# Moving the modulation steps of a streamed transformer kernel: out of the hybrid tail, into the dense, Mamba and mixture blocks

## The chip, the cores and the metric

The kernel runs on one core of one Trainium2 chip. The metric is the device time of one execution in microseconds; a comparison goes by the median of several executions.

## The reference

For 256 tokens of width 1024, in fp32, two chains of layers are computed one after the other. Every layer but the last norm is modulated by the condition vector c:

```python
def adaln(c, w, b):
    mod = jax.nn.silu(c) @ w + b
    shift, scale, gate = jnp.split(mod[:, None, :], 3, axis=-1)
    return shift, scale, gate

def modulate(x, norm_w, shift, scale):
    return rmsnorm(x, norm_w) * (1 + scale) + shift

for layer in range(DEPTH):                 # DEPTH = 2
    if layer % 2 == 0:
        mix = hybrid_mixer(modulate(x, ...), ...)     # GLA and NSA heads
        x = x + gate * mix
        x = x + gate * swiglu(modulate(x, ...), dense_w_gu, dense_w_down)
    else:
        x = x + gate * mamba2_mixer(modulate(x, ...), ...)
        x = x + gate * moe_ffn(modulate(x, ...), router, w_gu, w_down)   # 8 experts, top 2
return rmsnorm(x, final_norm)
```

After it come two layers of the second chain, each with a norm, a projection of width 4096, dilated and block attention, an output projection and a gate. So there are six modulations, mod0 to mod5 (hybrid, dense, Mamba, mixture, and the two second layers). Each is the product of silu(c) (1024) with a matrix of 1024 by 3072: the first 2048 columns are shift and scale, the last 1024 the gate.

## The kernel before

All weights are streamed from memory once, in chunks of 512 KB (128 partitions by 1024 numbers), through one ring of six buffers, by DMAs that the queue of SyncE (SP) issues in the order in which they were asked for. A weight chunk is called a half: ScalarE rounds it to the short format of the matmul (`split_scalar`, L503), VectorE subtracts to get the rest (`split_vector`, L515), and TensorE forms three products of high and low parts for every matmul (`mm3`, L526 to L528). Rounding and subtracting run up to SPLITS = 6 halves ahead of TensorE (`m + SPLITS` in the calls). A half of the dense block, of its down part and of the projections is twelve to 24 matmuls, one of the mixture six.

The modulations are not computed by matmuls of the stream but on VectorE. A modulation step multiplies one chunk of its matrix (128 rows by 1024 columns) by the matching 128 values of silu(c), one value per partition, and adds to an accumulator `macc` (`back_vector`, L579; the first step of each part, L576, only multiplies). A modulation has 24 such steps: 16 for shift and scale ("step"), 8 for the gate ("gate"). What is left is the sum over the 128 partitions, by TensorE with a matrix of ones (`back_tensor`): a "sum" entry of 16 columns of blocks (32 instructions) and a "gates" entry of 8 (16 instructions), each borrowing a PSUM bank; VectorE then adds the bias (L589, L591, L596, L599). All entries of the six modulations stand in one list, `Stream.back` (L400 to L408), in the order in which they must run; a few are "rest", which do nothing. The list is not tied to times. Both engines walk it with `back_steps(engine, k, name, n, limit)`, called at fixed places in their programs, n entries per call, and `back_until` runs it up to a named entry. On TensorE an entry of kind step, gate or rest costs nothing. So moving calls moves every later entry, and with it the load of the chunk, which takes its place in SP's order where VectorE's program asks for it. A chunk's buffer is free again when its step has run.

Where the list is walked, before:

- the hybrid block: one entry per half of the projection; then its tail, in which only the attention and GLA tracks ("live") run, two entries per round of the tracks, up to mod1's "gates" entry (L1070, L1164). Then the output projection with its sum entries, four halves with one entry each;
- the dense block (`dense_tensor` L1753, `dense_vector` L1864): a stage of gate and up weights per item j (11 items of two tiles), with 0, 2, 1, 1 entries in its four parts (`dense_back`), and, per unit of four tiles, a down-stage of four halves with one entry at every second half. At the start of the block the list is run up to mod1's gates, and the gate, a column per block, is turned to a row (`row_tensor`, 16 small matmuls). TensorE's items take two of the banks 4 to 7 (`turns.take`), freed by VectorE's product of up and silu(gate) (`up_vector`, L1828), which is followed by the low part of the operand (L1833); VectorE and ScalarE do this for item j - 1 behind a split in the stage of item j. The list stops there at BACK_PAUSE, the first gate entry of mod4;
- the Mamba block (`mamba_tensor`, `mamba_vector`): one entry per quarter of the first four items of SSM_ORDER, beside the convolution (taps L2163, activation L2147);
- the mixture (`moe_tensor` L2336, `moe_vector` L2435): none. An expert is 14 items of four halves; after every second item comes a down-stage of four halves. After an item TensorE turns the gated product that VectorE writes (L2688) with two transposes (`flip_tensor`), and the gather of the next expert runs from item 8 on;
- the second layers (`second_tensor` L3006, `second_vector`): one entry per quarter of the rounds (part 0 and 1, items i = 0 to 3), for layer 0 and for the part of layer 1 that still has entries. The last norms have fill matmuls (`norm_tensor`, NORM_FILL, `fill`): matmuls on constants whose result nobody reads, in place of idle time.

## Time and profile before

| | |
|---|---|
| time, median of 3 executions | 2112.31 us (2109.10 to 2114.84) |
| the profiled execution | 2110.27 us, span 2108.5 us |
| mean granted TensorE clock | 0.982 of full |
| TensorE (matmul) busy | 2007.5 us, 95% |
| VectorE busy | 1718.7 us, 82% |
| ScalarE busy | 1321.8 us, 63% |
| DMA | 560.19 MB, mean 266 GB/s |

The page of the profile gives the busy time per engine and the groups of instructions that cost most, each with its idle time before it and what ended that. Then the waits per engine and line say who waits for whom. The timeline of an engine, over a few microseconds, shows a line per run of like instructions, with the idle time ahead of it in brackets; the window table gives busy time, granted clock and DMA rate of a stretch. Names: `ring` is the buffer of a streamed chunk, `sph` and `spl` its high and low part, `ps` a PSUM bank, `macc` the accumulator of the modulations, `hH`, `hL`, `rH`, `rL` the high and low parts of operands, `arena` scratch. The blocks lie at about 30 to 228 us (hybrid), 230 to 440 (dense), 440 to 700 (Mamba), 720 to 1730 (mixture), 1730 to 1925 and 1925 to 2105 (second layers).

### The profile page before, as it was taken

The numbers are of one execution on the slowest core, as the hardware profiler recorded it, in microseconds if no ns is written. First come the engines' busy times: TensorE is split into PE (matmuls) and PEld (weight loads), VectorE is DVE, ScalarE is ACT, GpSimd is POOL, SyncE is SP. The second block draws the span as 40 slices with busy tenths as digits, with TensorE's granted clock in tenths as the row PEclk, the third lists the DMA queues.
The fourth block names the chain that finished last, engine by engine and source line by source line (L and its number), as shares of the span: only waits on it lengthen the run. The fifth ranks groups of instructions, "written<-read, shape, count | busy, mean of one in ns | idle before, by whom it ended". The sixth has DMA issues, their size and how long they took to land.

```text
span 2108.5 us, 28640 instructions
## 1 busy us (share of the span) xinstructions
PE 2007.5 (95%) x10424; PEld 1663.2 (79%) x10424; DVE 1718.7 (82%) x2427; ACT 1321.8 (63%) x1972; POOL 0.2 (0%) x4
## 2 busy tenths in 40 slices
PE   6998999998989999999999999999999999999997
PEld 5777889978877788888888888888788866767776
DVE  7688878768777698989899898998989988776664
ACT  4354534355564688778787777777778764544543
POOL 0000000000000000000000000000000000000000
PEclk9999999999999999999999999999999999999999
DMA  9846688846332399989999998999989984662530
GB/s 371 294 146 214 240 295 316 292 145 203 127 102 97 107 377 337 359 320 369 358 354 355 329 366 324 377 348 334 364 322 370 364 331 173 214 213 93 197 110 20
DMA packets 154211, 560.19 MB, mean 266 GB/s; under 512 B 17232, under 2 KB 17488, under 8 KB 153936
## 3 DMA queue, kind: packets, MB, share of 16 engines
q1 hardware_dynamic: 154064, 558.29, 72.6%
q8 instruction: 85, 1.39, 0.3%
q14 instruction: 62, 0.51, 0.1%
HBM read 557.18 MB, written 1.05 MB: 265 GB/s over the span
## 4 chain that ended last, share of the span: by engine, by line
PE 74%; DVE 14%; ACT 6%; issue 3%; DMA 3%; DVEq 0%; SPq 0%; ACTq 0%
PE ps L526 20%; PE ps L528 20%; PE ps L527 20%; PE ps L532 11%; DVE spl L515 7%; PE ps L536 3%; ACT sph L503 2%; DVE macc L579 1%; DMA ring<-in_moe_gu 1%; DMA ring<-in_dense_down 1%; DMA ring<-in_mod 1%; DMA ring<-in_moe_down 1%; ACT arena L2129 1%; ACT arena L770 1%; DVE arena L2163 0%
## 5 line engine op out<-in xcount | busy, mean ns | idle before, releaser
L515 DVE TENSOR_TENSOR spl<-ring,sph 128x1024 fp32r<-128x1024 f32 x906 | 1077.5, 1218 | 274.4 <-ACT sph L503 265.2
L503 ACT ACTIVATE sph<-ring 128x1024 fp32r<-128x1024 f32 x906 | 949.3, 1059 | 554.1 <-PE ps L528 407.5
L526 PE MATMUL ps<-sph,hH 128*128 128x512 f32 (+1 forms) x1296 | 520.3, 401 | 1.3 <-DVE hL L883 1.3
L528 PE MATMUL ps<-sph,hL 128*128 128x512 f32 (+1 forms) x1296 | 507.2, 391 | 0.0
L527 PE MATMUL ps<-spl,hH 128*128 128x512 f32 (+1 forms) x1296 | 505.8, 390 | 0.0
L526 PEld LDWEIGHTS ps<-sph,hH 128*128 128x128 f32 x1296 | 245.5, 189 | 51.5 <-issue 3.8
L528 PEld LDWEIGHTS ps<-sph,hL 128*128 128x128 f32 x1296 | 244.7, 189 | 52.5
L527 PEld LDWEIGHTS ps<-spl,hH 128*128 128x128 f32 x1296 | 245.5, 189 | 48.0 <-issue 1.0
L526 PE MATMUL ps<-sph,rH 128*128 128x512 f32 x664 | 269.9, 407 | 5.6 <-ACT arena L3117 2.0
L528 PE MATMUL ps<-sph,rL 128*128 128x512 f32 x664 | 260.8, 393 | 0.0
L527 PE MATMUL ps<-spl,rH 128*128 128x512 f32 x664 | 260.7, 393 | 0.0
L526 PE MATMUL ps<-hH,sph 128*128 128x256 f32 x640 | 185.7, 290 | 5.5 <-DVE arena L1182 3.6
L528 PE MATMUL ps<-hH,spl 128*128 128x256 f32 x640 | 183.1, 286 | 0.0
L527 PE MATMUL ps<-hL,sph 128*128 128x256 f32 x640 | 183.0, 286 | 0.0
L532 PE MATMUL ps<-arena 128*128 128x128 f32 (+6 forms) x940 | 147.7, 302 | 15.8 <-DVE arena L2322 9.2
L579 DVE SCALAR_TENSOR_TENSOR macc<-ring,st,macc 128x1024 f32<-128x1024 f32 x124 | 158.0, 1278 | 4.2 <-DMA ring<-in_mod 3.0
L526 PEld LDWEIGHTS ps<-sph,rH 128*128 128x128 f32 x664 | 126.0, 190 | 37.2 <-issue 3.1
L532 PEld LDWEIGHTS ps<-arena 128*128 128x128 f32 (+2 forms) x940 | 120.5, 194 | 39.9 <-issue 26.9
L536 PE MATMUL ps<-cst,arena 128*128 128x128 f32 (+2 forms) x640 | 114.5, 288 | 37.3 <-DVE arena L2688 13.1
L528 PEld LDWEIGHTS ps<-sph,rL 128*128 128x128 f32 x664 | 125.6, 189 | 27.3
L527 PEld LDWEIGHTS ps<-spl,rH 128*128 128x128 f32 x664 | 126.0, 190 | 25.5 <-issue 1.4
L536 PEld LDWEIGHTS ps<-cst,arena 128*128 128x128 f32 (+2 forms) x640 | 81.0, 147 | 80.6 <-issue 30.8
(313 smaller groups left out, 1766.9 us busy)
## 6 DMA issues: line engine op xcount, KB each, us to landing
ring<-in_moe_gu SPq DMA_DIRECT2D x448, 512.0 KB, 5.4
ring<-in_moe_down SPq DMA_DIRECT2D x224, 512.0 KB, 5.3
ring<-in_mod SPq DMA_DIRECT2D x144, 512.0 KB, 4.8
ring<-in_w_in SPq DMA_DIRECT2D x64, 512.0 KB, 4.3
ring<-in_dense_gu SPq DMA_DIRECT2D x44, 512.0 KB, 5.5
ring<-in_ssm_w_in SPq DMA_DIRECT2D x40, 512.0 KB, 3.4
ring<-in_dense_down SPq DMA_DIRECT2D x22, 512.0 KB, 5.6
ring<-in_hyb_w_in SPq DMA_DIRECT2D x20, 512.0 KB, 5.9
```

Source lines behind the costliest of these rows:

```text
L503: a.activation(k.high[m % SPLITS][:, 0:w], raw[:, 0:w], ACT.Copy).then_inc(k.S.half_rounded, 1)
L515: v.tensor_tensor(k.low[m % SPLITS][:, 0:w], raw[:, 0:w], k.high[m % SPLITS][:, 0:w], ALU.subtract).then_inc(*k.tick(k.S.half_split, f"hal ...
L526: pe.matmul(out, a[0], b[0], start=start, stop=False, skip_group_check=True)
L527: pe.matmul(out, a[0], b[1], start=False, stop=False, skip_group_check=True)
L528: return pe.matmul(out, a[1], b[0], start=False, stop=stop, skip_group_check=True)
L532: return pe.matmul(out, a, b, start=start, stop=stop, skip_group_check=True)
L536: return pe.transpose(out, in_, k.C["ident"][0:n, 0:n])
L579: v.scalar_tensor_tensor(out=m, in0=w[:, :], scalar=c, in1=m, op0=ALU.mult, op1=ALU.add).then_inc(*tick(S.mod_stepped, f"mod{i}.step{r}"))
L770: a.activation(k.norm_space.fulls[2 * t + h][:, j, :], bank[:, j * 128:(j + 1) * 128], ACT.Identity, bias=k.mods[:, i, c:c + 1], scale=k.m ...
L2129: a.activation(conv_slot(k, f), bank, ACT.Identity, bias=k.V["convb"][:, f:f + 1], scale=cw[:, f, 3:4]).then_inc(*tick(S.conv_in, f"ssm{j} ...
```

## The change

The list is the same but for one thing: mod1, like mod4, has three "rest" entries ahead of its sum, and its gate steps all come behind the sum. What moves are the calls:

- The hybrid tail stops at mod1's first gate entry instead of its "gates" entry. By the counts of the entries, ten steps run later than before.
- The gate's row of the dense block is not made at its start but behind item GATE_AT = 2 (list up to mod1's gates, then `gate_tensor` on banks 2 and 3 and `gate_scalar`), and the norm before has two fills in its place.
- The down-stages of the dense block call entries (0, 2, 1, 1) on TensorE and one per half on VectorE, so four per unit instead of two. In them the up product of VectorE and its part on ScalarE stand ahead of the split of the first half, not behind. The two fills ahead of the last down-stage go.
- In the Mamba block, the last quarter of an item has no entry, and the first item has two per quarter.
- The mixture has one entry per expert, behind item BACK_AT = 11.
- In the second layers, quarters 2 and 3 of the rounds with i = 1 have none.

In number of VectorE steps: ten fewer in the hybrid tail, eight more in the dense block, two more in the Mamba block, eight in the mixture, eight fewer in the second layers. The amount of arithmetic is unchanged, apart from four fill matmuls more at one place and four fewer at another.

```diff
--- before.py
+++ after.py
@@ -400,7 +400,7 @@
         self.back = []
         for i in range(6):
             steps, gates = [("step", i, r) for r in range(2 * KD)], [("gate", i, 2 * KD + r) for r in range(KD)]
-            late = [("rest", i, r) for r in range(3)] if i == 4 else gates[0:3]
+            late = [("rest", i, r) for r in range(3)] if i in (1, 4) else gates[0:3]
             if i == 0:
                 self.back += steps[0::2] + [("shift", 0, 0)] + steps[1::2] + [("sum", 0, 0)] + gates
                 continue
@@ -710,6 +710,8 @@
             fill(pe, k, banks, NORM_FILL[i])
     if i > 3:
         fill(pe, k, banks, 6 if i == 5 else 3)
+    if i == 1:
+        fill(pe, k, banks, 2)
     if i == 0:
         back_steps(pe, k, "tensor", 5)
         fill(pe, k, k.banks_turn, 1)
@@ -1067,7 +1069,7 @@
             live.append(gla_tensor(pe, k, linear, one))
     while live:
         advance(live)
-        back_steps(pe, k, "tensor", 2, ("gates", 1, 0))
+        back_steps(pe, k, "tensor", 2, ("gate", 1, 2 * KD))
     k.back_banks = one
     pe.wait_ge(*when("hyb.low2"))
     m = k.stream.first["hyb_out"]
@@ -1161,7 +1163,7 @@
             live.append(gla_vector(v, k))
     while live:
         advance(live)
-        back_steps(v, k, "vector", 2, ("gates", 1, 0))
+        back_steps(v, k, "vector", 2, ("gate", 1, 2 * KD))
     v.wait_ge(*k.when("dtw.high"))
     v.tensor_tensor(k.dtw3[:, :, 32:64], k.dtw[:, :, :], k.dtw3[:, :, 0:32], ALU.subtract).then_inc(*k.tick(k.S.vector_step, "dtw.low"))
     v.wait_ge(*k.when("row3.high"))
@@ -1750,12 +1752,14 @@
 
 
 
+
+GATE_AT = 2
+
+
 def dense_tensor(pe, k):
     S, tick, when = k.S, k.tick, k.when
     norm_tensor(pe, k, 1, k.banks_turn.only(4, 5, 6, 7))
     turns = k.back_banks = k.banks_turn.only(4, 5, 6, 7)
-    back_until(pe, k, "tensor", 1, "gates")
-    row_tensor(pe, k, "ffn.gate", k.mods[:, 1, 16:24], 8, ("mod1.gated",))
     acts = [[x[:, i * 1024:(i + 1) * 1024].rearrange("p (k n) -> p k n", k=4) for x in (k.rH, k.rL)] for i in range(2)]
     us, tail = units(DENSE_TILES), []
     for u in range(-1, len(us)):
@@ -1777,10 +1781,12 @@
                                            [x[:, n, :] for x in (k.hH, k.hL)], n == 0 and r == 0, n == 7)
                     last.then_inc(k.S.half_used, 1)
                     dense_back(pe, k, "tensor", part)
+                if j == GATE_AT:
+                    back_until(pe, k, "tensor", 1, "gates")
+                    for _ in gate_tensor(pe, k, "ffn", 1, k.banks_turn.only(2, 3)):
+                        pass
         if u >= 0:
             f, nt = us[u]
-            if u == len(us) - 1:
-                fill(pe, k, turns, 2)
             pe.wait_ge(*when(f"act{f + nt - 1}.low"))
             for kk in range(nt):
                 m = k.stream.at["dense_down", f // 2 + kk // 2] + kk % 2
@@ -1793,8 +1799,7 @@
                         out_banks(pe, k, "ffn", t)
                     last = out_product(pe, k, w, acts[u % 2], kk, t, f + kk == 0, False)
                 last.then_inc(k.S.half_used, 1)
-                if kk % 2 == 0:
-                    back_steps(pe, k, "tensor", 1, BACK_PAUSE)
+                back_steps(pe, k, "tensor", (0, 2, 1, 1)[kk], BACK_PAUSE)
     out_tail(pe, k, "ffn", tail)
 
 
@@ -1835,7 +1840,6 @@
 
 def dense_scalar(a, k):
     norm_scalar(a, k, 1)
-    row_scalar(a, k, "ffn.gate", k.F.gate, 8)
     us = units(DENSE_TILES)
     done = 0
     for u in range(-1, len(us)):
@@ -1847,6 +1851,9 @@
                     if part == 0 and done < j:
                         up_scalar(a, k, done)
                         done += 1
+                if j == GATE_AT:
+                    for _ in gate_scalar(a, k, "ffn", k.F.gate):
+                        pass
         if u == 0:
             rope_scalar(a, k)
         if u >= 0:
@@ -1854,16 +1861,15 @@
             for kk in range(nt):
                 if f + kk >= DENSE_TILES - 4:
                     break
-                split_scalar(a, k, k.stream.at["dense_down", f // 2 + kk // 2] + kk % 2 + SPLITS)
                 if kk == 0 and done < DENSE_TILES // 2 and k.stream.at["dense_gu", done] < k.stream.at["dense_down", f // 2]:
                     up_scalar(a, k, done)
                     done += 1
+                split_scalar(a, k, k.stream.at["dense_down", f // 2 + kk // 2] + kk % 2 + SPLITS)
     squares_scalar(a, k, "ffn", k.stream.first["ssm"], 2)
 
 
 def dense_vector(v, k):
     norm_vector(v, k, 1, "hyb")
-    back_until(v, k, "vector", 1, "gates")
     us = units(DENSE_TILES)
     done = 0
     for u in range(-1, len(us)):
@@ -1876,6 +1882,8 @@
                         up_vector(v, k, done)
                         done += 1
                     dense_back(v, k, "vector", part)
+                if j == GATE_AT:
+                    back_until(v, k, "vector", 1, "gates")
         if u == 0:
             rope_vector(v, k)
         if u >= 0:
@@ -1883,12 +1891,11 @@
             for kk in range(nt):
                 if f + kk >= DENSE_TILES - 4:
                     break
-                split_vector(v, k, k.stream.at["dense_down", f // 2 + kk // 2] + kk % 2 + SPLITS)
-                if kk % 2 == 0:
-                    back_steps(v, k, "vector", 1, BACK_PAUSE)
                 if kk == 0 and done < DENSE_TILES // 2 and k.stream.at["dense_gu", done] < k.stream.at["dense_down", f // 2]:
                     up_vector(v, k, done)
                     done += 1
+                split_vector(v, k, k.stream.at["dense_down", f // 2 + kk // 2] + kk % 2 + SPLITS)
+                back_steps(v, k, "vector", 1, BACK_PAUSE)
     add_vector(v, k, "ffn", k.stream.first["ssm"], k.F.gate, ("ffn.gate.copied4",), k.F.tmp, 2)
 
 
@@ -1929,8 +1936,8 @@
                                    c == 0, c == 7)
             last.then_inc(S.half_used, 1)
             advance(live)
-            if j in SSM_ORDER[0:4]:
-                back_steps(pe, k, "tensor", 1, BACK_PAUSE)
+            if j in SSM_ORDER[0:4] and q < 3:
+                back_steps(pe, k, "tensor", 2 if j == SSM_ORDER[0] else 1, BACK_PAUSE)
             if scan_starts(j, q):
                 live.append(scan_tensor(pe, k, beside))
         if j >= 4:
@@ -1996,8 +2003,8 @@
         for q in range(4):
             split_vector(v, k, m + q + SPLITS)
             advance(live)
-            if j in SSM_ORDER[0:4]:
-                back_steps(v, k, "vector", 1, BACK_PAUSE)
+            if j in SSM_ORDER[0:4] and q < 3:
+                back_steps(v, k, "vector", 2 if j == SSM_ORDER[0] else 1, BACK_PAUSE)
             if scan_starts(j, q):
                 live.append(scan_vector(v, k))
         if j >= 4:
@@ -2333,6 +2340,10 @@
 
 
 
+
+BACK_AT = 11
+
+
 def moe_tensor(pe, k):
     S, tick, when, E = k.S, k.tick, k.when, k.E
     norm_tensor(pe, k, 3, k.banks_turn.only(4, 5, 6, 7))
@@ -2383,6 +2394,8 @@
         if it == 8 and e + 1 < N_EXP:
             gather_now_tensor(pe, k, e + 1)
             live.append(gather_tensor(pe, k, e + 1))
+        if it == BACK_AT and e < N_EXP:
+            back_steps(pe, k, "tensor", 1)
         if it in (3, 6) and 1 <= e < N_EXP:
             scatter_tensor(pe, k, e - 1, it // 3 - 1)
     fill(pe, k, k.banks_turn, 3)
@@ -2469,6 +2482,8 @@
             shares_vector(v, k, e + 1)
         if it == 8 and e + 1 < N_EXP:
             live.append(gather_vector(v, k, e + 1))
+        if it == BACK_AT and e < N_EXP:
+            back_steps(v, k, "vector", 1)
         if it in (3, 6) and 1 <= e < N_EXP:
             live.append(scatter_vector(v, k, e - 1, it // 3 - 1))
         while q >= n_items - 1 and live:
@@ -3029,7 +3044,8 @@
                         last = second_product(pe, k, m, q, t, outs[t])
                     last.then_inc(k.S.half_used, 1)
                     advance(live)
-                    back_steps(pe, k, "tensor", 1)
+                    if i != 1 or q < 2:
+                        back_steps(pe, k, "tensor", 1)
             if part == 1 and i == 0:
                 back_until(pe, k, "tensor", 4 + l, "gates")
                 live.append(gate_tensor(pe, k, f"s{l}", 4 + l, beside))
@@ -3174,7 +3190,7 @@
             for q in range(4):
                 split_vector(v, k, m + q + SPLITS)
                 advance(live)
-                if part + i > 0:
+                if part + i > 0 and (i != 1 or q < 2):
                     back_steps(v, k, "vector", 1)
             if part == 1 and i == 0:
                 back_until(v, k, "vector", 4 + l, "gates")
```

## Rows read from the trace of the kernel before

**Rows 1.** The page: busy time by engine, and the chain of waits.

```profile
PE 2007.5 (95%) x10424; PEld 1663.2 (79%) x10424; DVE 1718.7 (82%) x2427; ACT 1321.8 (63%) x1972; POOL 0.2 (0%) x4
...
PE 74%; DVE 14%; ACT 6%; issue 3%; DMA 3%; DVEq 0%; SPq 0%; ACTq 0%
```

**Rows 2.** The page, costliest groups: count, busy, mean ns, idle before.

```profile
L515 DVE TENSOR_TENSOR spl<-ring,sph 128x1024 fp32r<-128x1024 f32 x906 | 1077.5, 1218 | 274.4 <-ACT sph L503 265.2
...
L503 ACT ACTIVATE sph<-ring 128x1024 fp32r<-128x1024 f32 x906 | 949.3, 1059 | 554.1 <-PE ps L528 407.5
...
L579 DVE SCALAR_TENSOR_TENSOR macc<-ring,st,macc 128x1024 f32<-128x1024 f32 x124 | 158.0, 1278 | 4.2 <-DMA ring<-in_mod 3.0
```

**Rows 3.** Windows table: length, busy us by engine (instructions), PEclk, DMA share, GB/s.

```profile
272.60:276.00 3.40, 3.35 (x15) 3.35 (x16) 2.73 (x5) 1.69 (x3) 0.00 (x0) 0.50 1.00 407
...
1965.60:1969.00 3.40, 3.40 (x11) 2.85 (x11) 2.84 (x3) 0.60 (x1) 0.00 (x0) 0.50 0.80 263
```

**Rows 4.** PE timeline, dense block: start, us, line, tiles, count, [idle before].

```profile
272.65 1.22 PE L532 MATMUL ps<-cst,macc 128*128 128x128 f32 x4 [2.07 <-DVE arena L1828]
...
313.05 0.71 PE L532 MATMUL ps<-cst,macc 128*128 128x128 f32 x4 [1.04 <-DVE arena L1828]
...
421.80 1.88 PE L532 MATMUL ps<-cst 128*128 128x512 f32 x4
424.48 0.50 PE L526 MATMUL ps<-sph,rH 128*128 128x512 f32 x1 [0.80 <-DVE rL L1833]
```

**Rows 5.** DVE timeline, hybrid tail.

```profile
187.82 1.28 DVE L579 SCALAR_TENSOR_TENSOR macc<-ring,st,macc 128x1024 f32<-128x1024 f32 x1
...
191.39 2.66 DVE L579 SCALAR_TENSOR_TENSOR macc<-ring,st,macc 128x1024 f32<-128x1024 f32 x2
```

**Rows 6.** PE timeline, start of the output projection and of the dense block.

```profile
195.31 0.50 PE L526 MATMUL ps<-sph,rH 128*128 128x512 f32 x1 [1.50 <-DVE rL L1225]
...
230.03 0.36 PE L526 MATMUL ps<-hH,sph 128*128 128x256 f32 x1 [1.02 <-DVE hL L883]
```

**Rows 7.** PE timeline, the sum before the last norm.

```profile
1920.93 3.73 PE L532 MATMUL ps<-cst,macc 128*128 128x128 f32 x32
```

**Rows 8.** DVE timeline, Mamba block.

```profile
473.72 1.28 DVE L579 SCALAR_TENSOR_TENSOR macc<-ring,st,macc 128x1024 f32<-128x1024 f32 x1
```

**Rows 9.** PE timeline, Mamba block.

```profile
477.03 0.30 PE L536 MATMUL ps<-cst,arena 128*128 128x128 f32 x1 [2.84 <-ACT arena L2147]
...
508.62 0.44 PE L536 MATMUL ps<-cst,arena 128*128 128x128 f32 x2 [1.07 <-DVE mods L589]
```

**Rows 10.** Windows table, a stretch of the mixture, columns of rows 3.

```profile
950.00:966.00 16.00, 16.00 (x74) 13.18 (x73) 15.47 (x17) 13.71 (x18) 0.00 (x0) 1.00 1.02 407
```

**Rows 11.** DVE timeline, mixture, the gated product.

```profile
961.06 0.41 DVE L2688 TENSOR_TENSOR arena<-arena,ps 128x256 f32<-128x256 f32 x1
```

**Rows 12.** PE timeline, mixture, the turns that take it.

```profile
962.45 0.38 PE L536 MATMUL ps<-cst,arena 128*128 128x128 f32 x2
```

**Rows 13.** All waits: engine, line, releaser: us in total, times, longest.

```profile
PE ps L536 <- DVE arena L3276: 6.5, 4, 1.9
```

**Rows 14.** PE timeline, second block.

```profile
1780.36 1.42 PE L536 MATMUL ps<-cst,arena 128*128 128x128 f32 x8 [1.84 <-DVE arena L3276]
...
1808.49 0.91 PE L532 MATMUL ps<-cst,macc 128*128 128x128 f32 x3 [1.31 <-DVE arena L1685]
...
1865.61 0.44 PE L536 MATMUL ps<-cst,arena 128*128 128x128 f32 x2
...
2034.23 1.03 PE L536 MATMUL ps<-cst,arena 128*128 128x128 f32 x6 [0.89 <-DVE arena L3276]
```

**Rows 15.** DVE timeline, second block.

```profile
1867.58 0.47 DVE L1685 SCALAR_TENSOR_TENSOR arena<-cst,ps 128x128 f32<-128x128 f32 x2
```

**Rows 16.** Windows table, a dense unit and an expert, as rows 3.

```profile
332.00:366.00 34.00, 34.00 (x242) 32.10 (x242) 28.10 (x30) 15.05 (x21) 0.00 (x0) 1.00 0.91 334
968.10:1094.10 126.00, 124.20 (x575) 102.21 (x575) 114.42 (x128) 99.72 (x127) 0.00 (x0) 1.00 0.93 349
```

## The prediction

> **What bounds the kernel now.** I first read the busy shares [rows 1]: TensorE 95%, VectorE 82%, and a chain of waits that is 74% TensorE, 14% VectorE and 3% DMA. The costliest groups with the idle time ahead of them [rows 2] say which of them is ahead: ScalarE's rounding of the weights (L503) waits 407.5 us for TensorE to use up a half, and VectorE's subtraction (L515) 265.2 us for that rounding. So the splitting of the streamed weights mostly runs ahead, six halves at most, and the end is set by TensorE. A microsecond taken off VectorE is worth something only where TensorE waits for that very operation, and one added costs something only where VectorE is late. Two quantities therefore carry the sum: TensorE's idle gaps, and the stretches at the lower of its two clocks [rows 3]: granted clock 0.50, that is 1.2 instead of 2.4 GHz, for 3.4 us each, each right behind an idle gap. The first lies behind the gap of 2.07 us that ends at 272.65 [rows 4]. Work that fills such a stretch takes twice as long, so it costs 3.4 / 2 = 1.7 us on top of the gap. Not every gap has one: behind the 1.04 us that end at 313.05 the same four matmuls took 0.71 us, behind the 2.07 us 1.22 [rows 4].
>
> The prices of the moved pieces: a modulation step takes VectorE 1.28 us, of which 0.08 overlap the next operation (so 1.20 in a queue), a weight split 1.22 [rows 2]. Each step also brings one 512 KB load on SP's queue, in the same ring of buffers as the weights: it holds a buffer until the step has run, and the weight loads asked for after it come one place later. Ten steps fewer in the tail, eight more in the dense block, two more in the Mamba block, eight in the mixture and eight fewer in the second block mean so many loads each; their number stays.
>
> **The hybrid tail.** Before, the tail's rounds issue two back-list entries each; the change stops at mod1's gates, so ten steps leave. The step at 187.82 stands between the sum and the attention's last operations; two more, at 191.39 to 194.05 [rows 5], stand ahead of the subtraction that makes the mixer's low part (L1225), for which TensorE waits 1.50 us before the output projection at 195.31 [rows 6]. One step of 1.2 us off the first chain and two off the second would be 3.7 us; TensorE's own transposes, which end 1.50 us before 195.31, are then next and move forward by the first of the steps alone: 1.5 + 1.2 = 2.7, less a little of the low clock that they run at, so I take 2.5 (bounds 1.5 and 3.1).
>
> **Entering the dense block.** The gate's 16 small matmuls and the row's 16 matmuls moved behind item 2. Before, the row's matmuls were followed by a wait for the normed input that runs on for 1.02 us more, to 230.03 [rows 6], so they were free; fills take their place. After, the row stands on the path, 16 of the small matmuls of which 32 take 3.73 us [rows 7]: -1.8. mod1's gates cost TensorE about as much in item 1 as they did in the output projection (16 such again), 0. Item 2's bank is taken later because VectorE's product now follows a split: -0.8. With the tail: 2.5 - 1.8 - 0.8 = **-0.1** (bounds -2.5 and +1.5).
>
> **Sums in the dense block.** TensorE waits 2.07 us at 272.65 and 1.04 us at 313.05 for a bank that VectorE's product L1828 frees [rows 4]; the first is followed by the low clock [rows 3]. That is 2.07 + 1.6 + 1.04 = 4.7 us. After, eight steps more run in the block (two entries more per down-stage), the products stand ahead of the splits, and the sums fall elsewhere: sum 2 at item 5, gates 2 at the start of item 6. One such wait of 1 to 2 us stays, I think, perhaps with a slow stretch: **+2.4** (1.0 to 4.0).
>
> **End of the dense block.** Four fill matmuls (1.88 us) and then 0.80 us of waiting for rL L1833 [rows 4]. The fill goes, and the operand is ready earlier since the product no longer waits behind a split: **+2.7** (if VectorE is still late, only 0.8 to 1.5 of it, since a removed fill then merely becomes idle time).
>
> **The Mamba block.** One step ends up ahead of the convolution's taps at 473.72 [rows 8], and TensorE waits 2.84 us at 477.03, with the low clock behind it; at 508.62 it waits 1.07 us for a sum's copy [rows 9]. After, the last quarter of each item has no step: 1.2 off the first wait, 1.1 off the second, and the slow stretch may go: 1.2 + 1.1 + 1.2 (of 1.7) = **+3.5** (2.3 to 4.0).
>
> **The mixture.** This is new work beside a tight loop: eight steps, one per expert after item 11's down splits. Around there the transfers are saturated (407 GB/s, DMA share 1.02, [rows 10]), one chunk of 524,288 bytes every 1.29 us. VectorE's gated product (L2688) ends at 961.06 + 0.41 = 961.47 and TensorE takes it at 962.45 without waiting: slack 0.98 us [rows 11, 12]. A step in front costs VectorE 1.20 and the chunk delays what lands behind it by one 1.29: per expert from 1.20 - 0.98 = 0.2 to 1.20 + 1.29 - 0.98 = 1.5 us. The upper end is a step that runs only after the late half; but VectorE can do it while that half lands, and then 1.29 - 0.98 = 0.3 is lost. I take 0.6, nearer to this overlap: 8 x 0.6 = **-5** (0 if the splits' lead covers it, -12 if nothing overlaps).
>
> **The second block.** Rounds 2 and 3 of item 1 lose their steps. TensorE's turns wait four times for VectorE's L3276, 6.5 us in all [rows 13]: 1.84 at 1780.36, 0.89 at 2034.23 where no steps run [rows 14], so 3.8 us in the two between, near 1853 and 1965. If these fall to 0.85 to 0.9 each, that is 3.8 - 1.75 = +2.05, and with the slow stretch at 1965.6 [rows 3], 1.65 of its 1.7, +3.7. The waits of 1.84 and of 1.31 at 1808.49 (for gates 4, [rows 14]) are each followed by a slow stretch too; the first shortens to 0.6 without its clock, the second moves behind the turns, 2.5 and its clock: 1.84 + 1.7 + 1.31 + 1.6 - 0.6 - 2.5 - 1.7 = +1.6 (-1 to +3). Against that, sum 5, 3.73 us at 1920.93 before a norm that waits anyway [rows 7], is now reached earlier in the list and lands in a saturated round: 3.75 us, plus a wait for a bank of pair 6, 7 until VectorE's L1685 ends at 1867.58 + 0.47 = 1868.05 [rows 15] (TensorE has its transposes behind it at 1865.61 + 0.44 = 1866.05, [rows 14]: 2.0), plus a slow stretch, 1.6: -7.4 (-5.8 if the clock holds). The norm's gap, now empty for 3.7 us, then lowers the clock for the turns behind it: -1.5 (0 to -3). Together 3.7 + 1.6 - 7.4 - 1.5 = **-3.6** (-7 to 0).
>
> **Sum.** -0.1 + 2.4 + 2.7 + 3.5 - 5 - 3.6 = -0.1 us saved. The profiled execution took 2110.27 us, 2.04 under the median 2112.31; 2110.3 + 0.1 + 2.0 gives **2112.3 us**. Its own range from the bounds, taken not all at once, is 2106 to 2118.
>
> **Rivals.**
> First, faster: no slack is missing in the mixture (0 instead of -5), sum 5 keeps its clock (+1.6), and the norm's fill keeps the clock (+1.5): 2112.3 - 8.1 = 2104, down to 2100. For it speaks that ScalarE is 407.5 us ahead as a whole [rows 2]; against it, the saturated transfers of [rows 10]. Chance 0.29.
> Second, slower, by one mechanism: the mixture's step delays the product by more than its 0.98 us of slack in every expert, and the half behind the chunk too. It decides from that 0.98 on: 8 x 1.5 = 12 instead of 5, which gives 2119.3; where the wait goes on to lower the clock once or twice, 2122. For it: VectorE is busy 15.47 of 16 us there [rows 10]; against: the step can run while the late half lands. Chance 0.20.
> Third, the transfers bind. A dense unit took 34 us, and its 334 GB/s are 21.7, so 22 chunks (12 halves, 10 steps); an expert took 126 us, and its GB/s are 84 chunks [rows 16]. Now they are 24 and 85. At 1.29 us [rows 10] that is 31.0 and 109.7 us, so they don't bind and it costs nothing. Were the expert's mean pace of 126 / 84 = 1.50 us all that there is, a unit would take 36.0 us, 2 longer, five times, and each expert 1.5 longer, 12 for the 5: 2112.3 + 10 + 7 = 2129. The window of [rows 10] speaks against it. Chance 0.03. By the Trainium skill's page "DMA: Bandwidth & Descriptors", section "Where 436 GB/s comes from", the memory side of a core is limited to about 358 GB/s, from which I estimate 1.46 us per chunk and 35.1 us for a dense unit; this trace disagrees, with 407 GB/s over 16 us.
> Fourth, the edits do not do what they say: steps pushed out of the tail simply come back where TensorE waits equally, so that all terms cancel: 2112, within 2. Chance 0.02.
>
> **Chances.** The forecast has 0.46. A measurement of this kernel tells about 0.3% (6.3 us) from no change. Faster by more than that (under 2106): 0.27 of the first rival and 0.04 of the forecast, 0.31. Slower (over 2118.6): 0.17 of the second, 0.03 of the third and 0.03 of the forecast, 0.23. The rest, 0.46, lies within. The range takes in the first rival to 2101 and the second to 2121, which leaves about a tenth on either side.
>
> **What would show it.** Right: no wait at the output projection's start near 193, no fill and no wait ahead of the last down-stage, waits at 474 and 508 shorter by 1.2 and 1.1; in the mixture a wait of 0.2 to 1.5 us at item 13 of each expert, ended by L2688; a sum of 32 instructions in the saturated round near 1867 with a wait ahead of it. Wrong: experts as long as before (126 us) would take the 5 us away; a norm 5 without the low clock 1.5; a sum 5 that is found elsewhere 7.4; expert lengths over 127.3 us would be the second rival; and dense units over 35 us the third.

## The result, and the profile after

The changed kernel takes 2117.43 us (median of 20 executions, 2110.41 to 2122.49) against 2109.35 us of the kernel before beside it (20 executions, 2102.70 to 2114.84): a ratio of 1.0034, 95% interval 1.0024 to 1.0044. It is slower by a third of a per cent, about 7 us. The prediction had said no change, 2112.3 us.

The profiled execution of the changed kernel took 2116.84 us, span 2115.1. Its page, for the busy time and the chain of waits:

```profile
PE 2003.9 (95%) x10424; PEld 1658.6 (78%) x10424; DVE 1718.6 (81%) x2427; ACT 1322.5 (63%) x1972; POOL 0.2 (0%) x4
...
PE 67%; DVE 17%; ACT 7%; DMA 6%; issue 3%; DVEq 0%; SPq 0%; ACTq 0%
```

TensorE's busy time fell by 3.6 us and VectorE's is the same as in [rows 1], so nothing is paid in work. What changed is the chain: TensorE's share of it went from 74 to 67%, VectorE's from 14 to 17%, and the DMAs' from 3 to 6%. By this chain, moved loads hold up TensorE more often.

Where the time went can be read without any model. Every kernel here issues the same 7800 weight matmuls (lines 526 to 528) in the same order, so the start of the n-th one can be laid beside that of the kernel before. The differences by stage, in us (a stage runs from the first weight matmul of one to the first of the next; "low" is the time at granted clock 0.5 in it):

| stage | before | low | changed | low | difference |
|---|---|---|---|---|---|
| hybrid block with its output projection | 193.8 | 17.1 | 191.2 | 20.5 | -2.6 |
| dense block up to its last four down halves | 194.4 | 3.4 | 198.5 | 6.8 | +4.1 |
| those four and the norm | 28.9 | 3.3 | 27.5 | 0.5 | -1.4 |
| Mamba block | 270.9 | 20.8 | 270.5 | 20.2 | -0.4 |
| mixture | 999.0 | 0.0 | 1006.9 | 0.0 | +7.9 |
| end of the mixture, norm 4 | 25.9 | 6.8 | 25.3 | 0.0 | -0.6 |
| first second layer, with norm 5 | 184.3 | 13.7 | 188.6 | 13.7 | +4.3 |
| last layer | 166.5 | 10.2 | 162.3 | 3.5 | -4.2 |

The mixture alone is as large as the whole loss. The changed kernel's timeline of TensorE at the places that the prediction spoke of (start, length, line, tiles, count, idle time before and what ended it):

```profile
192.08 0.79 PE L526 MATMUL ps<-sph,rH 128*128 128x512 f32 x1 [0.56 <-DVE rL L1227]
...
227.08 0.36 PE L526 MATMUL ps<-hH,sph 128*128 128x256 f32 x1 [1.09 <-DVE hL L885]
...
250.19 1.95 PE L532 MATMUL ps<-cst,macc 128*128 128x128 f32 x16
...
253.61 0.39 PE L526 MATMUL ps<-hH,sph 128*128 128x256 f32 x1 [1.47 <-DVE mods L596]
...
310.72 2.07 PE L532 MATMUL ps<-cst,macc 128*128 128x128 f32 x8 [3.87 <-DVE arena L1833]
```

The output projection starts at 192.08 instead of 195.31 (the first row of [rows 6]), after 0.56 us of waiting instead of 1.50. The last row is what replaced the two waits of [rows 4]: one of 3.87 us.

The granted clock at these places and around the last norms, in the table of windows (length, busy time of each engine, clock, DMA share, GB/s):

```profile
189.70:196.50 6.80, 6.24 (x19) 4.88 (x19) 2.54 (x5) 2.24 (x5) 0.00 (x0) 0.50 0.00 0
309.20:316.00 6.80, 5.28 (x25) 5.28 (x25) 3.78 (x6) 2.11 (x5) 0.00 (x0) 0.50 0.88 337
...
1872.50:1875.90 3.40, 3.40 (x18) 3.40 (x18) 0.00 (x0) 0.00 (x0) 0.00 (x0) 0.50 0.53 176
1933.50:1937.30 3.80, 0.36 (x3) 0.36 (x4) 3.56 (x12) 0.52 (x3) 0.00 (x0) 1.00 0.28 109
```

And in the second layers:

```profile
1785.64 1.25 PE L536 MATMUL ps<-cst,arena 128*128 128x128 f32 x8 [0.65 <-DVE arena L3292]
...
1789.17 2.50 PE L532 MATMUL ps<-cst,macc 128*128 128x128 f32 x16 [2.27 <-DVE arena L3294]
...
1857.29 0.93 PE L536 MATMUL ps<-cst,arena 128*128 128x128 f32 x5 [0.74 <-DVE arena L3292]
...
1871.56 5.47 PE L532 MATMUL ps<-cst,macc 128*128 128x128 f32 x32 [2.07 <-DVE arena L1687]
...
1936.94 1.60 PE L536 MATMUL ps<-cst,arena 128*128 128x128 f32 x8 [3.69 <-DVE arena L869]
```

The sum of mod5 stands at 1871.56: 2.07 us of waiting and 5.47 us for 32 instructions that took 3.73 in [rows 7], since the low clock of 1872.5 lies over them. Norm 5 now waits 3.69 us where the sum had been.

### The profile page after: what moved, and what is told of

It is laid out like the page before. It is cut to its first block, busy times and chain, and to the rows that moved or that the text cites. A ratio compares the mean times of both kernels' runs of the same rounds, so it can differ in the third digit from the quotient of the medians.

```text
span 2115.1 us, 28639 instructions
## 1 busy us (share of the span) xinstructions
PE 2003.9 (95%) x10424; PEld 1658.6 (78%) x10424; DVE 1718.6 (81%) x2427; ACT 1322.5 (63%) x1972; POOL 0.2 (0%) x4
## 4 chain that ended last, share of the span: by engine, by line
PE 67%; DVE 17%; ACT 7%; DMA 6%; issue 3%; DVEq 0%; SPq 0%; ACTq 0%
PE ps L526 18%; PE ps L528 17%; PE ps L527 17%; PE ps L532 11%; DVE spl L515 9%; ACT sph L503 3%; PE ps L536 3%; DMA ring<-in_moe_down 3%; DMA ring<-in_moe_gu 2%; DVE macc L579 1%; DMA ring<-in_mod 1%; DVE arena L2170 1%; DMA ring<-in_dense_gu 1%; DVE arena L2703 0%; ACT arena L2136 0%
## 5 line engine op out<-in xcount | busy, mean ns | idle before, releaser
L526 PE MATMUL ps<-sph,rH 128*128 128x512 f32 x664 | 270.6, 408 | 4.5 <-ACT arena L3133 2.0
L527 PEld LDWEIGHTS ps<-spl,rH 128*128 128x128 f32 x664 | 126.4, 190 | 25.5 <-issue 1.4
```

The costliest lines, as they stand in the source:

```text
L526: pe.matmul(out, a[0], b[0], start=start, stop=False, skip_group_check=True)
L527: pe.matmul(out, a[0], b[1], start=False, stop=False, skip_group_check=True)
```

## The experiments

All ratios are to the kernel before, of the same batch, with their 95% intervals. The stages of all of them, as above, in us, each from one profiled execution:

| kernel | hybrid | dense | + norm | Mamba | mixture | norm 4 | layer 1 | layer 2 |
|---|---|---|---|---|---|---|---|---|
| before | 193.8 | 194.4 | 28.9 | 270.9 | 999.0 | 25.9 | 184.3 | 166.5 |
| changed | 191.2 | 198.5 | 27.5 | 270.5 | 1006.9 | 25.3 | 188.6 | 162.3 |
| x1, no mixture steps | 193.2 | 198.7 | 27.3 | 270.6 | 1000.2 | 25.5 | 178.0 | 164.9 |
| x2, sum 5 held | 190.0 | 198.0 | 27.3 | 270.7 | 1006.5 | 25.4 | 178.2 | 166.1 |
| x3, two steps per down-stage | 189.4 | 190.3 | 29.1 | 270.3 | 1004.1 | 28.1 | 184.1 | 166.4 |
| x4, order and fills alone | 196.6 | 189.3 | 30.0 | 270.8 | 999.8 | 26.0 | 184.1 | 164.9 |
| y1, steps spread in the items | 189.8 | 194.7 | 29.7 | 272.5 | 999.3 | 25.8 | 184.1 | 166.4 |
| y2, Mamba block's calls alone | 195.1 | 193.0 | 27.5 | 270.3 | 998.6 | 25.8 | 184.2 | 165.1 |
| y3, short operation | 193.7 | 198.7 | 27.5 | 270.4 | 1008.7 | 25.6 | 189.9 | 162.3 |
| y4, short load | 191.2 | 198.6 | 30.3 | 271.1 | 1005.6 | 25.0 | 189.6 | 160.6 |
| y5, mixture steps at item 7 | 189.6 | 198.7 | 30.1 | 270.0 | 1001.8 | 25.5 | 188.5 | 162.4 |
| z1, y3 and y4 together | 187.7 | 196.9 | 28.5 | 268.3 | 1010.1 | 26.0 | 188.5 | 162.2 |
| z4, y1 with free banks | 191.5 | 194.7 | 30.2 | 268.3 | 999.9 | 24.6 | 184.1 | 166.5 |
| z5, y5 and x2 | 189.9 | 197.3 | 28.5 | 268.4 | 1001.4 | 26.1 | 179.4 | 166.0 |

Rows that should agree show how far one profile can be trusted: the mixture without steps 998.6 to 1000.2, the hybrid stage of the changed kernel's code 187.7 to 193.7, by where the low clock falls.

### The mixture's steps: are they the loss?

```diff
-        if it == BACK_AT and e < N_EXP:
-            back_steps(pe, k, "tensor", 1)
...
-                    if i != 1 or q < 2:
-                        back_steps(pe, k, "tensor", 1)
+                    back_steps(pe, k, "tensor", 1)
```

(and the same for VectorE)

> The changed kernel without its eight steps in the mixture; the second layers get their steps in all quarters back, as before. Theory: in the changed kernel TensorE falls behind the kernel before by 8.1 us within the mixture (its weight matmuls start 0.98 us earlier than before at 593 us and 7.17 us later at 1730 us), and each step is the cause of that. Without them the mixture keeps the distance that it enters with, about -1 us, and the run ends about 1 us under before (between -3 and +1). Rival: the loss comes from a changed order of the ring's loads that the earlier blocks leave behind, not from the steps; then the mixture still loses 6 to 8 us and the run ends 5 to 8 us over before.

Measured: 2107.22 us, ratio 0.9977 (0.9961 to 0.9992). The mixture takes 1000.2 us: 6.7 of its 7.9 us are gone. The rival falls. The run is better than the theory said, 4.9 instead of 1 us under before, because of the first second layer, 178.0 us against 184.3. That is not the edit: its list and its waits there are those of the kernel before, and only the clock differs, as the part on the hardware below shows. About 6 of this profile's gain are therefore the clock's, and it isn't this execution alone: the median of the granted clock is 0.982 in its eight executions and 0.980 in the 29 of before (the table at the end).

### What does a step cost there: the operation, the load, or its place?

TensorE's waits for the gated product between 720 and 1735 us (us in total, times, longest), first of the kernel before, then of the changed one, and then item 13 of the second and the third expert in the changed kernel:

```profile
PE ps L536 <- DVE arena L2688: 13.1, 14, 1.2
```

```profile
PE ps L536 <- DVE arena L2703: 18.3, 21, 1.4
```

```profile
962.99 0.41 PE L536 MATMUL ps<-cst,arena 128*128 128x128 f32 x2 [0.65 <-DVE arena L2703]
...
1090.73 0.41 PE L536 MATMUL ps<-cst,arena 128*128 128x128 f32 x2 [1.37 <-DVE arena L2703]
```

Seven waits more for eight steps, and 5.2 us more of waiting out of the 7.9 lost. The first of the two shown stands where [rows 12] had none, and both are as long as the prediction had them (0.2 to 1.5). To tell apart what makes them, seven of the eight steps were cut down, one respect at a time (what these three kernels compute for mod4's gate is then not the reference's, and each was executed once):

```diff
-            v.scalar_tensor_tensor(out=m, in0=w[:, :], scalar=c, in1=m, ...)
+            n_ = 64 if i == 4 and kind == "gate" else QUARTER
+            v.scalar_tensor_tensor(out=m[:, 0:n_], in0=w[:, 0:n_], scalar=c, in1=m[:, 0:n_], ...)
```

> The changed kernel with seven of the eight modulation steps in the mixture working on 64 of their 1024 columns (the rest of that gate's sums is left out): VectorE's time for them almost goes, their loads stay. The stretch from the first to the last weight matmul of the mixture takes 999.0 us in the kernel before and 1006.9 in the changed one. Theory A, VectorE's own 1.2 us per step are the cost: it falls to 999 to 1001. Theory B, the load that delays the halves behind it by 1.29 us is the cost: it stays at 1005 to 1007.

Measured: the mixture takes 1008.7 us, 3.5 us of it at the low clock, which costs 1.7; without that 1007.0. The short operation (0.28 us instead of 1.28) has saved nothing. Theory A falls.

```diff
-        k.stream.ask(("mod", i, r), mod[r], QUARTER, f"mod{i}.step{r}")
+        slim = 64 if i == 4 and kind == "gate" and r != 2 * KD else QUARTER
+        k.stream.ask(("mod", i, r), mod[r][:, 0:slim], slim, f"mod{i}.step{r}")
```

> The changed kernel with seven of the eight modulation chunks in the mixture cut to 64 of 1024 columns in the load alone (the step works on whole rows of the buffer, so its result is not the reference's): VectorE's time stays, the transfer almost goes. Theory A (VectorE's time): the mixture stays at 1005 to 1007 us. Theory B (the load): it falls to 999 to 1001. If both halves of the cost count, each of the two runs lies in between, near 1003.

Measured: 1005.6 us. The short load saves 1.3 of 7.9 us. Theory B, that the transfer is the cost, falls too (the prediction had charged the operation and the transfer together).

> The changed kernel with seven of the eight mixture steps short in both respects: 64 of 1024 columns loaded and 64 worked on (that gate's sums are not the reference's). What is left of a step is its place in the ring of six buffers and in SP's and VectorE's order. With the short operation alone the mixture took 1008.7 us, with the short load alone 1005.6, as it stood 1006.9, without steps 999.0 to 1000.2. Theory C, the place is the cost (a buffer that holds no weights, so that the loads run one half less ahead in the stretch in which they catch up): 1004 to 1007. Theory D, operation and load hide each other's absence, either alone is enough to make the product late: 999 to 1002.

Measured, with both cuts: 1010.1 us, with 3.5 us of low clock, so 1008.4 without; the waits for the gated product are 20.0 us. Theory D falls, and C is what is left: neither the operation nor the bytes are the cost, so by elimination it is the place in the ring and in the order of loads. ScalarE's rounding in this kernel, behind the shortened load of the second expert:

```profile
948.89 1.06 ACT L503 ACTIVATE sph<-ring 128x1024 fp32r<-128x1024 f32 x1 [0.32 <-DMA ring<-in_moe_gu]
950.50 1.06 ACT L503 ACTIVATE sph<-ring 128x1024 fp32r<-128x1024 f32 x1 [0.55 <-DMA ring<-in_moe_gu]
952.73 1.06 ACT L503 ACTIVATE sph<-ring 128x1024 fp32r<-128x1024 f32 x1 [1.17 <-DMA ring<-in_moe_down]
954.42 1.06 ACT L503 ACTIVATE sph<-ring 128x1024 fp32r<-128x1024 f32 x1 [0.64 <-DMA ring<-in_moe_down]
```

It waits 1.17 us for a half although almost no bytes stood ahead of it, and the starts are 1.61, 2.23 and 1.69 us apart, where at the 407 GB/s of [rows 10] one half lands every 1.29. A half takes 5.4 us from issue to landing (the page's median), and a buffer is loaded again only when its step has run. That shows in the changed kernel at the second expert's step: SP issues its load, VectorE runs the step, and SP issues the load six places later into the same buffer.

```profile
948.26 0.33 SPq L485 DMA_DIRECT2D ring<-in_mod  x1
```

```profile
954.78 1.28 DVE L579 SCALAR_TENSOR_TENSOR macc<-ring,st,macc 128x1024 f32<-128x1024 f32 x1
```

```profile
956.09 0.33 SPq L485 DMA_DIRECT2D ring<-in_moe_down  x1
```

The step ends at 956.06 and the load is issued 0.03 us later; so it is at all eight steps. The buffer was away from the weights for 7.8 us. With both cuts it still was, for 7.0 us (issue at 943.27, end of the step at 950.27), because a load of a sixteenth of the bytes took 4.4 us instead of 5.2 (the medians of the modulation's loads in this kernel's list of DMAs) and the step waits its turn behind VectorE's splits. With one of six buffers holding no weights for so long, too few loads are under way to follow each other without a gap in the stretch in which the stream catches up. This last link is argued from the rows, no run varied the number of buffers.

```diff
-BACK_AT = 11
+BACK_AT = 7
```

> The changed kernel with the mixture's step behind item 7 instead of item 11. Theory: what it costs depends on where VectorE and the transfers are late; items 11 to 13 lie in the stretch in which the loads catch up after the gather of the next expert, item 7 lies ahead of the gather. The mixture then takes 999 to 1002 us instead of 1006.9, and the run is 4 to 7 us faster than the changed kernel. Rival: VectorE is equally full in every item, so each step costs its 1 us anywhere: 1005 to 1007.

Measured: 2110.95 us, ratio 1.0007 (0.9992 to 1.0023), mixture 1001.8 us, waits for the gated product:

```profile
PE ps L536 <- DVE arena L2703: 15.0, 15, 1.5
```

Fifteen waits instead of 21. The same eight steps cost 1.6 to 3.2 us ahead of the gather (over the 998.6 to 1000.2 without them) and 6.7 to 8.3 in the catching up behind it. The theory holds.

### The dense block: how many loads beside a down-stage?

In the changed kernel ScalarE waits for the down halves just ahead of the wait of 3.87 us:

```profile
302.16 1.06 ACT L503 ACTIVATE sph<-ring 128x1024 fp32r<-128x1024 f32 x1 [2.78 <-DMA ring<-in_dense_down]
305.46 1.06 ACT L503 ACTIVATE sph<-ring 128x1024 fp32r<-128x1024 f32 x1 [2.24 <-DMA ring<-in_dense_down]
308.02 1.06 ACT L503 ACTIVATE sph<-ring 128x1024 fp32r<-128x1024 f32 x1 [1.50 <-DMA ring<-in_dense_down]
```

Their starts are 3.30 and 2.56 us apart: a down half and a step's chunk take turns, each 1.29 us of transfer at the pace of [rows 10]. VectorE's product waits in its queue behind the splits of these halves, and it frees the bank that mod2's sum borrows.

```diff
-                back_steps(pe, k, "tensor", (0, 2, 1, 1)[kk], BACK_PAUSE)
+                if kk % 2 == 0:
+                    back_steps(pe, k, "tensor", 1, BACK_PAUSE)
```

> The changed kernel with two steps instead of four in each down-stage of the dense block (as before), and the second layers' steps in all quarters, which take up those that are left. The mixture's steps stay. Theory: in the changed kernel TensorE waits 3.87 us at 310.7 us for a bank, after ScalarE waited 2.78, 2.24 and 1.50 us for three down halves whose loads stand behind the steps' loads; the low clock behind it costs 2.6 us more. With two steps per stage that wait is at most 2 us and the dense block ends 4 to 6 us earlier; the mixture still loses 6 to 8 us; the run ends 1 to 4 us over before. Rival: the wait comes from where the sum falls, not from the number of loads; then it stays at 3 us or more and the dense block wins less than 2 us.

(The same on VectorE, and the second layers have their steps in all quarters again. In this kernel the steps of mod4 that are left over run in the mixture on an accumulator that holds other rows there, so the last layers' modulation is not the reference's.) Measured: 2108.97 us, ratio 0.9986 (0.9972 to 0.9999). The dense block takes 190.3 us instead of 198.5, more than the 4 to 6 expected: 1.9 of it is mod3's gates entry, which falls into the Mamba block, 3.4 the 6.8 us of low clock that are missing, and the rest the wait. The whole run is 3 us under before where 1 to 4 over was expected, and its mixture, with its steps, takes 1004.1 us, 1 under the least expected. TensorE's waits in the block (230 to 430 us) are then

```profile
PE ps L526 <- DVE mods L596: 1.5, 1, 1.5
```

and none for the product any more. By its own mark, a wait of 3 us or more that stays, the rival falls. But this kernel doesn't part the two theories by itself, since with fewer calls mod2's sum moves too: it stands behind the 1128th weight matmul, in the changed kernel behind the 1104th. The kernels with two steps per down-stage and an entry at that very place help. Before, mod2's gates stand behind the 1104th and wait 1.04 us for the same product [rows 4]; in x4 below, which has the product ahead of the split as the changed kernel has it,

```profile
313.33 2.05 PE L532 MATMUL ps<-cst,macc 128*128 128x128 f32 x16 [0.58 <-DVE arena L1826]
```

0.58 us, against 3.87 with four. So the place alone doesn't make the wait, and the number of loads beside it is what differs.

```diff
-                split_vector(v, k, ... dense_down ...)
-                if kk % 2 == 0:
-                    back_steps(v, k, "vector", 1, BACK_PAUSE)
                 if kk == 0 and done < DENSE_TILES // 2 and ...:
                     up_vector(v, k, done)
                     done += 1
+                split_vector(v, k, ... dense_down ...)
+                if kk % 2 == 0:
+                    back_steps(v, k, "vector", 1, BACK_PAUSE)
...
-            if u == len(us) - 1:
-                fill(pe, k, turns, 2)
```

> The kernel before with two edits of the change alone: in the down-stages the product stands ahead of the split, and the two fills ahead of the last down-stage are gone. Theory: the 1.88 us of fills and the 0.80 us of waiting at 424 us both go, and the waits for the product at 272 and 313 us shorten by a split each: 3 to 5 us under before. Rival: the fills covered a wait that is there anyway: the last down-stage starts at most 1 us earlier, and the run is within 1 us of before.

Measured: 2109.21 us, ratio 0.9992 (0.9979 to 1.0005), 1.7 us under before and not clear of it. That is less than the 3 to 5 of the theory. The dense stage does take 189.3 instead of 194.4 us, 1.7 of which are a low stretch that is missing, and the last down-stage starts with neither fill nor wait, so the rival falls; the waits for the product became 1.63 and 0.58 us instead of 2.07 and 1.04. But the stages on either side are 2.8 and 1.1 us longer, with 6.8 and 2.2 us more of low clock. The part works where it is made; as a whole it can't be told from the clock's scatter by the time alone. With the low clock taken out (the table at the end) it is worth 3.6 us.

```diff
-def dense_back(e, k, name, part):
-    back_steps(e, k, name, (0, 2, 1, 1)[part], BACK_PAUSE)
+def dense_back(e, k, name, part, j):
+    back_steps(e, k, name, (1 if j > 1 else 0, 2, 1, 1)[part], BACK_PAUSE)
```

(the same on VectorE, on top of x1 and x3)

> The changed kernel without steps in the mixture, two steps per down-stage as before, and instead one step more in the first quarter of the dense block's items 2 to 10; the second layers as before. Theory: what hurt in the dense block was four extra loads beside the four halves of a down-stage with the list's sum right behind it; spread over the items, the steps cost little: the dense block takes 190 to 193 us (194.4 before, 198.5 changed, 190.3 with two steps per down-stage and no others), and the run is 5 to 9 us under before. Rival: the block as a whole has no room for the loads (nine chunks in an item's 11.5 us are the full pace of 1.28 us): dense 196 us or more, and the run is no better than without the mixture's steps alone, 5 us under before.

Measured: 2105.40 us, ratio 0.9971 (0.9953 to 0.9988), 6.1 us under before. The dense block takes 194.7 us, over the 190 to 193 of the theory and under the rival's 196; the work is that of the changed kernel's 198.5. What spreading took away is above all the wait of 3.87 us and the low clock behind it: x1 and the changed kernel have 6.8 us of low clock in the stage, 3.4 us of time, and y1 has none. Without that the stage takes 195.1 to 195.3 us concentrated, 194.7 spread and 192.7 in the kernel before. So the steps aren't free anywhere in the block: ScalarE still waits 21.3 us for the items' loads (15.2 before), and TensorE has a new wait of 1.5 us for the copy of mod2's sum (L589).

(on top of y1)

```diff
-    turns = k.back_banks = k.banks_turn.only(4, 5, 6, 7)
+    turns, k.back_banks = k.banks_turn.only(4, 5, 6, 7), k.banks_turn.only(2, 3)
...
+                    k.back_banks = turns        # behind item GATE_AT
```

> The kernel with the steps spread over the dense block's items and none in the mixture, and with mod1's gates entry borrowing one of the banks 2 and 3, which nobody uses yet, instead of one of the items' four. Theory: TensorE's wait of 1.4 us for the copy of the gates (L596) behind the entry is a wait for a bank that the next item needs, so it goes with the bank: dense block 193.3 instead of 194.7 us, the run 1.4 us faster than with the spread alone, 6 to 8 us under before. Rival: the item then waits for its own product as long: nothing gained, 5 to 6 us under before.

Measured: 2104.40 us, ratio 0.9970 (0.9954 to 0.9985). The gates entry stands alone now,

```profile
250.93 1.95 PE L532 MATMUL ps<-cst,macc 128*128 128x128 f32 x16
```

with no wait before or behind it, and the block's waits are 3.7 instead of 4.9 us; so the wait for L596 was one for a bank. The stage is as long as in y1 (194.7), since a low stretch of 3.5 us lies in it, and the ratio can't be told from that of y1. The mechanism is shown, a gain in time is not.

### The second layers and the Mamba block

```diff
-                        back_steps(pe, k, "tensor", 1)
+                        back_steps(pe, k, "tensor", 1, ("sum", 5, 0) if l == 0 else None)
```

> The changed kernel, but the walk of the list in the first of the second layers stops in front of mod5's sum, which then runs ahead of the last norm, as before. Theory: the sum costs 7.4 us where the changed kernel has it (2.07 us of waiting for a bank at 1869 us, 3.75 us of work, 1.6 us of low clock) and is free in the norm's gap, where TensorE now waits 3.7 us: 5 to 7 us faster than the changed kernel, 0 to 2 us over before. Rival: the entries behind the sum, three gate steps, now fall into the next layer beside its own work and cost there what was won, and the wait for a bank goes to another borrower: under 3 us faster than the changed kernel, 4 or more over before.

Measured: 2109.78 us, ratio 0.9993 (0.9980 to 1.0005): from 1.0034 by 0.41%, 8.7 us, 4 to 14 from end to end of the two intervals, where 5 to 7 were expected. TensorE at norm 5:

```profile
1918.94 3.73 PE L532 MATMUL ps<-cst,macc 128*128 128x128 f32 x32
1922.51 2.74 PE L532 MATMUL ps<-cst 128*128 128x512 f32 x6
1925.37 1.09 PE L536 MATMUL ps<-cst,arena 128*128 128x128 f32 x8
```

Sum, fills and turns follow each other, and nothing waits. Layer 1 is 10.4 us shorter, 5.2 of it by 10.3 us less of low clock; layer 2 gives 3.8 back, of which 1.7 by the clock and 1.9 by a wait for a bank at mod5's gates. So the rival saw one thing rightly, and the theory holds; 3.5 of the 6.6 us that the two layers gained are the clock's.

> The changed kernel with two places mended: the mixture's step behind item 7, and mod5's sum held for the norm's gap. Theory: both gains add, since they lie in different blocks: 5 us from the mixture (1001.8 instead of 1006.9 us) and 6 us from the second layers, 2117.4 - 11 = 2106, that is 3 to 5 us under before. Rival: one of them comes back elsewhere, and the run is not clearly faster than before (within 2 us).

Measured: 2105.11 us, ratio 0.9970 (0.9953 to 0.9987), 6.3 us under before, a little more than the 3 to 5 expected. Mixture 1001.4, layer 1 179.4: both gains are there, in their own stages. This is the whole change with two of its places mended, and it is faster than the kernel before by as much as y1 and z4. In all three that is mostly the granted clock: without its part they lie 0.7 and 1.5 under and 1.6 over the kernel before (the table at the end).

```diff
-            if j in SSM_ORDER[0:4]:
-                back_steps(pe, k, "tensor", 1, BACK_PAUSE)
+            if j in SSM_ORDER[0:4] and q < 3:
+                back_steps(pe, k, "tensor", 2 if j == SSM_ORDER[0] else 1, BACK_PAUSE)
```

> The kernel before with the Mamba block's slots of the change alone (none in a last quarter, two in the first item's quarters). Theory: the wait of 2.84 us for the convolution shrinks by the step's 1.2, and the 1.07 us for the sum's copy go, but a later convolution that the sum's 3.7 us covered now shows a wait of about 1.8 us: the waits of the block stay within 1 us of the 15.6 us of before (as in the changed kernel, where they are 15.6 too), and the block gains under 1 us. Rival (the prediction): the waits go for good, the block's waits fall to 12 or 13 us and it gains 2.3 to 4.

Measured in the stage up to the scan, in the one execution: 139.4 us against 139.7 (139.1 in the changed kernel), waits 14.5 against 15.6 us. The gain under 1 us is as the theory had it, and the rival's 12 to 13 us of waits and gain of 2.3 to 4 are not there. But the theory's reason does not show in this kernel. Its sum of mod4 stands behind the same weight matmul as before, the 2160th, so it uncovers nothing, and no wait of 1.8 us appears. The first wait shrinks by 0.76 us and the one for the sum's copy goes,

```profile
476.02 0.39 PE L536 MATMUL ps<-cst,arena 128*128 128x128 f32 x1 [2.08 <-ACT arena L2147]
```

a wait of 0.78 for VectorE's L2069 is new, and the rest is lost to a low stretch of 6.8 us at 588.7 where before had 3.4 at 593.5.

In the changed kernel, whose list lags two entries further, three of the six waits for the convolution and the sum behind them are

```profile
476.05 0.30 PE L536 MATMUL ps<-cst,arena 128*128 128x128 f32 x1 [1.65 <-ACT arena L2154]
...
486.83 0.30 PE L536 MATMUL ps<-cst,arena 128*128 128x128 f32 x1 [1.20 <-ACT arena L2154]
...
503.28 0.41 PE L536 MATMUL ps<-cst,arena 128*128 128x128 f32 x2 [1.76 <-ACT arena L2154]
...
506.62 3.74 PE L532 MATMUL ps<-cst,macc 128*128 128x128 f32 x32
```

The first is 1.2 us shorter than in [rows 9], by just the step that left. The third did not exist: before, the sum of mod4, 3.7 us of TensorE's work, stood in front of the convolution's turns; with the sum two halves later the wait is in the open. That the sum had covered it is read from these two traces, no run moved the sum alone. By the start of the same weight matmuls the changed kernel gained 2.1 us up to the 2112th (that first wait and the low stretch of 477.4, which is missing), kept 1.45 behind the sum, and gave 1.0 back at 589, where a low stretch of 6.8 us stands instead of 3.4.

## Why the prediction was wrong

The time lies in the range (2101 to 2121) but on the slow side of the 0.3% that I had given 0.46; 2112.3 is 5.1 us under the median, and 7.2 us by the ratio, since the kernel before was itself 3.0 us faster beside it than in the executions that the forecast started from. Point by point, in saved microseconds:

1. **Hybrid tail and entry.** Forecast -0.1. The tail is right: the projection starts 3.2 us earlier (2.5 forecast, bound 3.1). But by 267 us, behind the gate's row, it has lost more than that: its weight matmuls are 2.26 us behind before, 2.6 against the lead of 0.35 that it began with. Most of that is the clock: the low stretch fell on the projection's matmuls and not on the transposes (window 189.7 to 196.5), which costs 2.0 more in this execution and nothing in six of the other kernels with this tail. The step that failed is the bank at 0.8: the gates entry brings a wait of 1.47 us, since the next item needs the bank that it borrowed (z4 removes the wait by other banks).
2. **Sums in the dense block.** The largest miss. Forecast +2.4 with one wait of 1 to 2 us left; that wait is 3.87 us, with 6.8 us of low clock over it. Measured -1.4 (the distance to before grows from 2.26 us at 267 to 3.69 at 420 us). I looked at the order of VectorE's operations and took the transfers as free since a whole unit needs 31 of its 34 us. The bound holds for the unit and fails within it: four chunks, two of them added, stand beside the four down halves, and what waits is the product behind them. The third rival had the right resource, and I had dismissed it by a mean.
3. **End of the dense block.** Forecast +2.7, measured +2.6 (from 3.69 to 1.11 us behind at the last down-stage, which starts with neither a fill nor a wait). Right.
4. **Mamba block.** Forecast +3.5, measured +0.4. The two waits did shrink, by 1.2 and 1.1, and the low stretch of 477.4 went. The step left out what is late next: 1.76 us for the convolution that the sum had stood in front of, 0.75 for VectorE's L2076, and 1.0 for the longer low stretch at 589.
5. **Mixture.** Forecast -5, range 0 to -12, measured -7.9. Place, form and size of the waits (0.65 to 1.37 us) are as written; their cause is not. I charged VectorE's 1.20 and the load's 1.29 us; with either or both cut the mixture still takes 1005.6 to 1008.4 us, so what is left is the buffer's place. The second rival went by the same two prices, and is no nearer.
6. **Second layers.** Forecast -3.6, measured +0.5 with norm 4. The sum of mod5 cost 2.07 + 5.47 = 7.54 us (7.4 forecast) and the turns' waits for L3292 fell from 6.5 to 2.8 us, 0.65 to 0.8 each where 0.6 and 0.85 to 0.9 were forecast. What I had not counted is the clock: 13.5 us less of low time in norm 4 and the last layer, 6.7 us at half price; the low stretch behind norm 5's gap came (1937.3), its neighbour of before at 1965 did not.

The sum of the misses: -2.5 (1), -3.8 (2), -0.1 (3), -3.1 (4), -2.9 (5), against +4.1 (6) and +1.4 behind the dense block, which is the clock's (3.3 us of it before, 0.5 after), as the 4.1 are too. The four losses go the same way, each a price of zero or near it for something that wasn't on TensorE's or VectorE's queue in the trace of before: a bank, a buffer, a covered latency. The step that failed, in short: the moved loads were taken to cost nothing in the dense block and 0.6 us each in the mixture, and the runs show a wait of 3.87 us with its low clock in the one and 1.0 us each, held by the ring's buffer, in the other. With the low clock taken out of all executions (the table at the end) the changed kernel is about 10 us slower; some 3 of them a higher granted clock gave back, which the forecast had not. That the time keeps 4 us from the upper end of the range is owed to that, and so is luck.

The third rival's limit as such did not show. The changed kernel's window over the catching up:

```profile
951.00:967.00 16.00, 15.35 (x70) 12.33 (x69) 15.57 (x17) 12.73 (x17) 0.00 (x0) 1.00 1.01 394
```

That is 394 GB/s, with a step's chunk among the halves. The Trainium skill's page "HBM Reference", section "Specifications (TRN2)", says that a core that streams alone measures well above its share of the pair's bandwidth. This trace agrees: its 394 GB/s are above the 358 of such a share that the prediction cites.

## What to carry to other kernels

In this kernel a moved step cost a buffer of the ring for as long as its chunk lay in it, and with a sixteenth of the bytes and of the operation it cost as much: put such a step where the stream has caught up, not beside the halves that are late. Check the transfers stage by stage and not by the mean of a block, and for each sum or fill that is moved, name the latency that it covered and the bank that it will borrow. Whoever compares single profiles should subtract the low clock first; laying the n-th weight matmul of two kernels side by side then shows each stage's share to about a microsecond.
